# Attention rows divided on ScalarE ahead of transposes, and a mixer loop ordered from other durations

## The reference

```python
proj = rmsnorm(x, norm1_w) @ w_in
o_a  = gated_delta_rule(qa, ka, va, g, beta)        # 4 heads of 128 channels
o_b  = dilated_attention(qb, kb, vb)                # 8 heads of 64 channels
x = x + concatenate([gated o_a, o_b]) @ w_out
x = x + (silu(gate) * up) @ w_down                  # after norm, w_up and a 3-tap conv
```

## Time and profile before

| | us |
|---|---|
| median of 3 runs | 2656.86 (2655.59 to 2659.09) |
| the profiled execution | 2655.63 |
| its span | 2654.0 |
| PE busy in the span | 2536.4 (96%) |
| DVE busy | 1506.7 (57%) |
| ACT busy | 1061.4 (40%) |

### The profile page before, as it was taken

The page is one execution under the profiler, slowest core; times in us unless marked ns, Lnnn a source line. Parts: engine busy times, 40 slices in busy tenths (PEclk is TensorE's granted clock), DMA queues, the critical chain, the costliest instruction groups (busy, mean ns, idle before and its releaser), DMA issues.

```text
span 2654.0 us, 36131 instructions
## 1 busy us (share of the span) xinstructions
PE 2536.4 (96%) x14218; PEld 2078.6 (78%) x14218; DVE 1506.7 (57%) x2521; ACT 1061.4 (40%) x1715; POOL 67.2 (3%) x118
## 2 busy tenths in 40 slices
PE   6999988999989999999999999979999999999997
PEld 4878866777768788888788888868888788888886
DVE  4114325656536666665648964476588755655555
ACT  3123323544534534444544454443334433423332
POOL 1000000000000000000000000000000000000000
PEclk9999998999999999999999999999999999999999
DMA  5322212111034455556444555522333333333331
GB/s 187 96 80 89 86 67 95 45 36 55 2 119 129 153 184 198 197 197 204 152 134 128 168 173 175 159 72 82 93 88 88 89 107 90 103 114 100 96 96 64
DMA packets 318470, 304.35 MB, mean 115 GB/s; under 512 B 10223, under 2 KB 277860, under 8 KB 318180
## 3 DMA queue, kind: packets, MB, share of 16 engines
q1 hardware_dynamic: 303332, 243.92, 31.4%
q0 software_dynamic: 14976, 58.20, 5.4%
HBM read 244.41 MB, written 57.67 MB: 114 GB/s over the span
## 4 chain that ended last, share of the span: by engine, by line
PE 84%; DVE 8%; ACT 3%; issue 3%; DMA 2%; SPq 0%; POOLq 0%; POOL 0%; DVEq 0%; ACTq 0%
PE PS L2020 13%; PE PS L2021 13%; PE PS L2022 13%; PE PS L1726 11%; PE PS L2037 6%; PE PS L2039 6%; PE PS L2038 6%; PE PS L1967 3%; PE PS L1851 3%; PE PS L1979 1%; PE PS L1837 1%; PE PS L1955 1%; DVE wl L1276 1%; DVE cg L1673 1%; ACT wh L939 1%
## 5 line engine op out<-in xcount | busy, mean ns | idle before, releaser
L2020 PE MATMUL PS<-hh,wh 128*128 128x512 f32 x1728 | 682.7, 395 | 4.3 <-DVE wl L1276 1.9
L2022 PE MATMUL PS<-hh,wl 128*128 128x512 f32 x1728 | 672.9, 389 | 0.0
L2021 PE MATMUL PS<-hl,wh 128*128 128x512 f32 x1728 | 672.5, 389 | 0.0
L939 ACT ACTIVATE wh<-raw 128x1024 fp32r<-128x1024 f32 x352 | 366.7, 1055 | 514.2 <-PE PS L2039 381.1
L1276 DVE TENSOR_TENSOR wl<-raw,wh 128x1024 fp32r<-128x1024 f32 x286 | 347.8, 1227 | 390.2 <-ACT wh L939 389.9
L1569 DVE TENSOR_TENSOR x<-x,PS 128x512 f32<-128x512 f32 x432 | 293.8, 685 | 180.9 <-PE PS L2039 180.1
L2020 PEld LDWEIGHTS PS<-hh,wh 128*128 128x128 f32 x1728 | 324.5, 188 | 76.8 <-issue 5.0
L2021 PEld LDWEIGHTS PS<-hl,wh 128*128 128x128 f32 x1728 | 324.5, 188 | 70.6 <-issue 4.6
L2022 PEld LDWEIGHTS PS<-hh,wl 128*128 128x128 f32 x1728 | 324.3, 188 | 67.8
L2037 PE MATMUL PS<-fh,wh 128*128 128x512 f32 x864 | 344.2, 398 | 18.7 <-DVE x L1569 10.9
L2038 PE MATMUL PS<-fl,wh 128*128 128x512 f32 x864 | 339.4, 393 | 0.0
(11 more groups left out here) (292 smaller groups left out, 2547.8 us busy)
## 6 DMA issues: line engine op xcount, KB each, us to landing
raw<-in_w_ff SPq DMA_DIRECT2D x128, 512.0 KB, 4.0
raw<-in_w_up SPq DMA_DIRECT2D x88, 512.0 KB, 4.4
wl_s<-wl POOLq DMA_DIRECT2D x66, 512.0 KB, 5.4
wl<-wl_s SPq DMA_DIRECT2D x66, 512.0 KB, 3.6
raw<-in_w_in SPq DMA_DIRECT2D x60, 512.0 KB, 4.0
raw<-in_w_down SPq DMA_DIRECT2D x44, 512.0 KB, 5.1
raw<-in_w_out SPq DMA_DIRECT2D x32, 512.0 KB, 3.9
qkvz_s<-st POOLq DMA_DIRECT2D x16, 512.0 KB, 2.9
```

What stands on the lines that cost most here:

```text
L939: A(whs(slot), raw[:, k % 2], ACT.Copy).then_inc(s["w_hi"], 1)
L2020: mm(bank, wh[:, k % 4, cut], hh[:, kk, span(a_)], start=kk == 0, stop=False)
L2021: mm(bank, wh[:, k % 4, cut], hl[:, kk, span(a_)], start=False, stop=False)
L2022: last = mm(bank, wl[:, k % 4, cut], hh[:, kk, span(a_)], start=False, stop=kk == KT - 1)
```

## The change

Three things.

1. The stage `dg` is replaced by `rd` (DVE: the reciprocal alone) and by `nm` for each head e (ACT: the row of weights, up to 128x1024, copied onto itself with that head's reciprocal as scale). `dgt` and its 2 KB per partition go.
2. `tr` turns the blocks with `nc.tensor.transpose` against the identity in place of the matmul by `dgt`, and waits for both `nm` of its tile.
3. `BUSY` and `NEAR` get other numbers, so that `place()` gives all three engines another order over the whole loop.

```diff
-            "kS": 0.5, "u": 0.5, "o": 1.0, "SU": 0.5, "ot": 0.5, "vt": 1.0,
+            "kS": 0.95, "u": 0.95, "o": 1.85, "SU": 0.95, "ot": 0.5, "vt": 0.95,
...
-                put("dg", c, j, after=[("exp", c, j, 1), ("tr", *two_before, last_of(two_before[1]))])
+                put("rd", c, j, after=[("exp", c, j, e) for e in range(2)])
+                for e in range(2):
+                    put("nm", c, j, e, after=[("rd", c, j)])
+                    self.BUSY["nm", c, j, e] = 0.05 + 0.131 * self.keys(c, j, m)[2] / P
...
-            put("tr", c, j, m, after=[("dg", c, j)] + ([("pt", *step_before, e) for e in range(2)] if step_before else []))
-            self.BUSY["tr", c, j, m] = 0.05 + 0.224 * w
+            put("tr", c, j, m, after=[("nm", c, j, e) for e in range(2)] + ([("pt", *step_before, e) for e in range(2)] if step_before else []))
+            self.BUSY["tr", c, j, m] = 0.05 + 0.22 * w
...
-            self.BUSY["pv", c, j, m] = 0.15 + 0.115 * w
+            self.BUSY["pv", c, j, m] = 0.15 + 0.21 * w
...
-    NEAR = 0.25
+    NEAR = 0.1
...
-            dgt = sb("dgt", [P, 2, 2, P], where=z)
...
+                elif name == "nm":
+                    j, e = stage[2:]
+                    n = mixers.keys(c, j, 0)[2]
+                    act.wait_ge(s["rd_ready"], 4 * c + j + 1)
+                    A(soft(j)[:, e, 0:n], soft(j)[:, e, 0:n], ACT.Copy, scale=ac[:, 3, 2 * j + e:2 * j + e + 1])\
+                        .then_inc(s["s_even"], 1)
...
-                elif name == "dg":
+                elif name == "rd":
                     j = stage[2]
                     dve.wait_ge(s["s_exp"], 8 * c + 2 * j + 2)
-                    done(V_.reciprocal(ac[:, 3, 2 * j:2 * j + 2], ac[:, 2, 2 * j:2 * j + 2]))
...
-                    for e in range(2):
-                        last = TS(dgt[:, j % 2, e], ident[:], ac[:, 3, 2 * j + e:2 * j + e + 1], None, ALU.mult)
-                    last.then_inc(s["dg_ready"], 1)
+                    V_.reciprocal(ac[:, 3, 2 * j:2 * j + 2], ac[:, 2, 2 * j:2 * j + 2]).then_inc(s["rd_ready"], 1)
...
-                    pe.wait_ge(s["dg_ready"], 4 * c + j + 1)
+                    pe.wait_ge(s["s_even"], 8 * c + 2 * j + 2)
...
-                            last = mm(PS[:, 5 + e, b - lo:b - lo + P], soft(j)[:, e, b:b + P], dgt[:, j % 2, e], start=True, stop=True)
+                            last = tr(PS[:, 5 + e, b - lo:b - lo + P], soft(j)[:, e, b:b + P], ident[:])
```

More of the change, by code:

```diff
@@ L353 @@
     TILES = (4, 7, 0, 3), (5, 6, 1, 2)
-    BUSY = {"gc": 0.5, "kk": 0.5, "cor": 0.36, "join": 0.6, "cor6": 0.3, "join6": 0.3, "qk": 0.5, "kT": 0.5, "vT": 0.5,
[5 rows of a table removed]
+    BUSY = {"gc": 0.95, "kk": 0.95, "cor": 0.6, "join": 1.05, "cor6": 0.55, "join6": 0.55, "qk": 0.95, "kT": 0.5, "vT": 0.5,
[5 rows of a table added]
     ON = {"pe": "gc kk cor join qk kT vT kS u o SU ot vt sc tr pv".split(),
-          "dve": "D LT U T AT v qd r St ov orec on og lo ttr mx dg blo".split(),
-          "act": "gam E half cp6 ke uc sq osd oh vb exp pt bhi".split()}
+          "dve": "D LT U T AT v qd r St ov orec on og lo ttr mx rd blo".split(),
+          "act": "gam E half cp6 ke uc sq osd oh vb exp nm pt bhi".split()}
     def __init__(self):
@@ L443, in attention @@
             put("sc", c, j, m, after=free + ([("vb", c)] if c % 2 == 0 and (j, m) == (0, 0) else []))
-            self.BUSY["sc", c, j, m] = 0.1 + 0.11 * w
+            self.BUSY["sc", c, j, m] = 0.12 + 0.215 * w
             for e in range(2):
                 put("ttr", c, j, m, e, after=[("sc", c, j, m)] + ([("tr", *two_before, last_of(two_before[1]))] if m == 0 else []))
-                self.BUSY["ttr", c, j, m, e] = 0.15 + 0.134 * w
+                self.BUSY["ttr", c, j, m, e] = 0.14 + 0.134 * w
             if m == last_of(j):
@@ L702, in program @@
             o_sq o_v o_sd o_r on_ready ot_mm og_ready oh_ready ol_ready
-            vt_mm vb_ready s_mm s_max s_neg s_exp dg_ready p_mm p_evac pv_mm b_hi b_lo
+            vt_mm vb_ready s_mm s_max s_neg s_exp rd_ready s_even p_mm p_evac pv_mm b_hi b_lo
             x_done u_evac f_one f_two f_silu a_f a_hi a_lo r_relu d_mm q_sq q_acc q_cols q_v q_sd q_diag q_spread q_R
```

## The result

The changed kernel takes 2598.87 us (median of 4 runs, 2597.07 to 2599.83) against 2656.23 us before (4 runs): a ratio of 0.9783, 95% interval 0.9766 to 0.9800, or -57.4 us. The forecast was 2630 with a range of 2612 to 2648. The profiled execution has a span of 2598.2 us, 55.8 less.

What follows compares the result with a forecast made beforehand. The prediction took PE to bound the mixer loop's body, with a 21 us tail bound by a chain over PE, ACT and DVE. -32.4 + 3 + 5 - 2 = -26.4 us from 2656.9 gave 2630 us, range 2612 to 2648.

Steps and rivals of the forecast that it cites:

- The transposes: PE in the mixer loop: 288 blocks at 0.11 instead of 0.2225 us, -32.4 us, 4.05 a chunk.
- The scaling on ACT and the way from `exp` to `tr`: Mixer loop: 64 nm add 49.4 us of ACT work, mostly hidden by PE's pace; +3 us on the path.
- the wide bounds, 0 and +34: Longer way from exp to tr: +1.06 us a tile over 32 tiles, from fully hidden to fully paid.
- The other order: New stage order in the loop: +5 us idle time in the body, -2 for the clock in the tail.
- 229.4 / 6 = 38.2 us a chunk: Period between gc of chunks 1 and 7, forecast to fall to 34.1, against 29.2 for the recurrence's chain.
- less filler must raise the idle time: Loop body: 10% less work to fill PE's gaps while U and T run, +5 us on 18.4 idle.
- The new order also saves idle time: Rival: better fit takes 10 us of the body's idle time and 6 of the tail's; some 2608, chance 0.10.
- The recurrence takes over: Rival: the recurrence's chain, delayed behind attention work and longer ACT rows, sets part of the pace; 2641, chance 0.18.
- ACT sets the pace: Rival: the added ACT work lies on the tile's path in full, +17 us; 2674, chance 0.08.
- the clock falls: Rival: transposes don't count as work for the clock, twelve falls to the lower level cost 25 us; 2655, chance 0.04.
- the -2 us that I took for the clock there: Loop's tail: -2 us, of 2.1 us that tr loses there to the lower clock.
- nothing there: Start to 415 us, phases 1 and 3, SP's and POOL's queues: same instructions in the same order, no change.

Runs made afterwards that it cites:

- e9: Changed kernel's operations, planned with the old BUSY table and NEAR = 0.25, but rd and nm at their new durations: 2622.23 us, ratio 0.9879.
- e1: Kernel before's operations (dg, tr as matmul by dgt, no nm) in the changed kernel's order on all three engines: 2630.45 us, ratio 0.9906.
- e3: Changed kernel with tr as ordinary matmuls by the identity in place of transposes, nm kept: 2629.54 us, ratio 0.9904.
- e8: Changed kernel in its own order with nm left out, tr waiting for the reciprocal instead: 2596.23 us, ratio 0.9780.
- e2: Changed kernel's operations in the kernel before's order, nm inserted at the place the old plan's times give: 2641.64 us, ratio 0.9949.
- e11: Kernel before's operations, planned with the new table and NEAR = 0.1, tr and dg at the durations in its trace: 2622.42 us, ratio 0.9877.
- e10: Changed kernel planned with the old, halved durations of the recurrence's PE stages, all else new: 2611.92 us, ratio 0.9838.
- e5: Changed kernel with NEAR = 0.25 as before, all other numbers of the new table kept: 2606.08 us, ratio 0.9815.
- e7: Changed kernel planned with the old, too short durations of sc and pv: 2601.34 us, ratio 0.9798.
- e6: Changed kernel with NEAR = 0, all other numbers kept: 2602.75 us, ratio 0.9803.
- e4: Changed kernel with every nm done twice, a plain copy of the row ahead of the scaled one: 2617.22 us, ratio 0.9857.

## Why the prediction was wrong

*The transposes* (-32.4): right. It is the larger part of what the operations give when they are planned, 32.8 us (e9). Between e1 and the changed kernel only the operations differ: PE's busy time goes from 324.3 to 292.1, 32.2 less, and the median by 31.6. e3 gives 30.7 the other way. The rest of that step, 4.05 us less in each chunk, rests on the period that fails below: it fell by 2.5.

*The scaling on ACT and the way from `exp` to `tr`* (49.4 us of work, 3 on the path): the rows of `nm` sum to 46.5 us, ACT's busy time grew by 43.1, and the path took some 3 (e8). In the old order, made without `nm`, the waits for it are 20.3 us (e2), so the wide bounds, 0 and +34, had a reason. What I had not seen is that the term belongs to the pair of order and operations; I took the old kernel's 2 waits of 32 as if the new order inherited them. That the 3 came out is therefore luck in part.

*The other order* (+5 in the body, -2 in the tail, together +3): this step failed. It measures -24.7 with the old operations put into it (e1), -32.6 when it is planned for them (e11), and -23.4 with the new operations (e9 against the changed kernel). Three things were wrong in it.

First, the period. "229.4 / 6 = 38.2 us a chunk" was taken as a chunk's work, and 94% busy as no room. But of each chunk's attention only a part was done in it. The last `gc` stood in the earlier trace rows at 670.84 and the loop's end in the earlier trace rows at 766.37, 95.5 us apart, and I read only the last 21 of them, as "a tail". The useful quotient was the loop by chunks, (766.4 - 394.4) / 8 = 46.5 us, beside what PE's work needs.

Second, the size of the room. I reasoned that less filler must raise the idle time: +5. PE's idle time in the loop went from 29.9 to 13.3. With the new table it is 7.7 for the old operations (e11), where there is the most filler, and 13.3 for the new ones, so the direction of that argument holds, by 5.6 us, and is the small part. The large part is that the old plan believed the recurrence's stages on PE to take half their time. e10 puts that alone at 13.1 us, up to 4.4 of it by the clock, NEAR at 7.2 (e5), the durations of `sc` and `pv` at 2.5 (e7), and all with the rest at 23.4 (e9). These are single orders, each with small differences of its own, and no run shows by which stages a halved duration makes PE wait: the wait for `U` comes back in e5 as well, where the table is the new one. The backlog itself, which I then took for the cause, isn't it: e5 has before's and loses 7, e6 has the shortest and gains nothing.

Third, I held busy time for work. With the same instructions PE is busy 6.0 us less in e1 and 8.2 less in e11 than before, over each whole loop (the 7.2 and 9.5 of the windows from 405 us include that those loops began 1.2 and 1.6 us earlier):

```profile
394.40:766.40 372.00, 336.30 (x4417) 275.58 (x4417) 208.18 (x785) 169.35 (x436) 1.01 (x3) 0.96 0.14 43
...
393.20:740.60 347.40, 330.25 (x4417) 272.62 (x4417) 208.08 (x785) 169.81 (x436) 1.00 (x3) 0.97 0.15 47
...
392.80:734.70 341.90, 328.12 (x4417) 271.98 (x4417) 209.73 (x785) 168.56 (x436) 0.99 (x3) 0.97 0.15 47
```

PE was busy 18.1 us at the lower level in the loop before, 11.2 in e1 and 10.5 in e11. At half the clock, half of the difference is an estimate of what the clock adds: 3.4 and 3.8 us. The other 2.6 and 4.4 us may be the seams between stages, which the view counts as busy, since the records overlap (288 ns each, 0.111 us apart); no run isolates it.

*The rivals.* "The new order also saves idle time" (2608, 0.10) was the nearest. Its reason, a table with half the true durations, is borne out by e9 and e10, and it was still 9 us short (its own terms, -50.4, make 2606.5). It took the long `tr` as its example; the durations that e10 finds to matter are those of the recurrence. I gave it little because of "94%", the reading that failed. "The recurrence takes over", "ACT sets the pace" and "the clock falls" did not occur. ACT is at 199.5 of 282 us, 71% as computed; with the rows doubled (e4, 79% over the loop) it does cost.

*The clock.* The grant is 1.00 from 415 to 697 us with the 288 transposes in it. The rule of the Trainium skill, "TensorE: Matmul & The Clock Gate", "Part 4: PE-mode transpose", as the prediction's rival read it, would have made the loop lose clock; the trace doesn't agree, at this mixture with matmuls. The fall comes with the idle tail, as before, and now reaches into phase 3:

```profile
697.00:705.00 8.00, 4.99 (x52) 3.90 (x50) 4.25 (x17) 7.69 (x22) 0.00 (x0) 1.00 0.00 1
705.00:716.00 11.00, 9.12 (x39) 6.99 (x40) 1.19 (x3) 2.06 (x6) 0.23 (x2) 0.54 0.38 122
```

PE was busy 5.0 of 8 us ahead of the fall. Of the lower level 4.4 us lie in the loop (706.0 to 710.4) in place of 6.8, and phase 3 is no longer for it (1887.8 us, before 1887.6). So of the -2 us that I took for the clock there at most 1.4 came, by the busy time in the two stretches (5.5 and 2.7 us). Another gain, for which the forecast had "nothing there", lies at the start: the lower level ended 3.4 us earlier.

```profile
394.50:412.40 17.90, 10.19 (x37) 7.47 (x37) 4.21 (x14) 2.03 (x3) 0.99 (x2) 0.50 1.00 329
412.50:416.00 3.50, 3.30 (x62) 2.64 (x62) 3.01 (x16) 1.80 (x5) 0.00 (x0) 1.00 0.09 33
```

In the kernel before it lasted to 415.8:

```profile
394.40:415.80 21.40, 12.56 (x60) 9.32 (x62) 5.81 (x20) 2.18 (x4) 0.99 (x2) 0.50 0.86 283
```

How much of the 4.2 us ahead of the second `gc` this makes is not isolated.

## What to carry to other kernels

Where two strands share engines, ask at each marker of the one how far the other is; a period is a chunk's work only if both have done a chunk. Where a planner's table is half off from the distances in the trace, its order is a term of its own, and not a small one even at 94% busy: here it was worth about as much as the saved matmul passes (23.4 to 32.6 us against 31.6), and of the durations put back it was those of the dependent chain that cost (e10), while two of the filler's (e7) did not. An added stage has to be in the plan: put into the finished order it cost 19 us more. And to split a gain between an order and its operations, plan each corner anew; an order made for other operations misstates both parts.

## What the runs showed of the hardware

An fp32 transpose of 128x128 takes 0.11 us in a row and an fp32 matmul of that size 0.2225, and 288 of them, turned back into matmuls in e3, cost 30.7 us, 0.107 each, on a PE that is busy 96% of its loop. The body of the loop, with 288 more transposes in it, kept the full clock (1.00 from 415 to 697 us). In e10 it fell to the lower level for 10.2 us behind 3.5 us in which PE was busy 1.6.
